# Merging the last projection with its mixer, packing the gates, and regrouping the sample value products

## The chip, the cores and the metric

One Trainium2 chip, one core, one launch of the whole program. The metric is the device time of one execution in microseconds (us), median of three runs. TensorE does the matrix products, VectorE, ScalarE and GpSimd (POOL) the element work, and SyncE starts most DMA transfers.

## The reference

One inference step of a two-layer decoder for a prompt of 256 tokens and 8 sample sequences of 4 tokens each, 288 token columns in all. Every sub-layer is `x = x + c * rmsnorm(f(rmsnorm(x)))`. Layer 0 is a half feed-forward, a mixer AB (sparse attention with a paged key/value cache, beside an RWKV-7 recurrence), and a half feed-forward; layer 1 has the mixer CD between its two feed-forwards. What the change touches, cut down:

```python
# CD mixer: retention (C) beside mLSTM (D)
z = h @ cd_w_in            # qc, kc, vc, gc, qkd, vd, ig, fg, og
qc, kc = rope(qc), rope(kc) * DK_C ** -0.5
ret_S, yc = chunked_scan(retention_chunk, ret_S, (qc, kc, vc))
qkd = silu(causal_conv(qkd)); qd, kd = split(qkd)
logi, logf = ig + b0, log_sigmoid(fg + b1)
(mC, mn, mm), hd = chunked_scan(mlstm_chunk, (mC, mn, mm), (qd, kd, vd, logi, logf))
y = concat(head_norm(yc) * silu(gc), head_norm(hd) * sigmoid(og)) @ cd_w_out
# AB mixer, sample side: p over 1024 cached and 4 new keys of each of 8 sequences
out = einsum('bqhk,bqkhd->bqhd', p, v_cached_and_new)
```

## The kernel before

Activations stand as `[128 features, 8 tiles, 288 tokens]`. A product with a weight matrix is three products of split fp32 numbers (`three_products`, lines 187 to 189): the high part of a weight by the high part of x, high by low, low by high. Weights come as "pairs" (128 x 2048 numbers, 1 MB, two output tiles of 128 features) through a ring of four slots. VectorE splits each pair (`split_pair`: a cast at line 173 and a subtraction at line 182), counted by the semaphore `pair_split`; TensorE counts the pairs it is done with in `pair_done`, and SyncE loads the next pair into a slot when that count allows.

The last projection (`cd_in_stage`) runs in one block with the stages ahead of it: eight pairs give `z` (18 tiles), then `project_values` gives the values of C and D in token-major form, each of two pairs and three token tiles (128, 128 and 32 tokens) of 24 products, and the thirteenth pair gives the eight gate rows, padded to two whole tiles of 128 features. Then the block ends with a barrier of all engines, and `cd_mix_stage` runs as a block of its own. Its order is written by hand, the same for each engine every time: gates' first steps, rotation of q and k (`rot`, line 2444 on TensorE, lines 2226 to 2228 on VectorE), the gates' scans up to `gate_arg`, the scores of C (lines 2451 and 2252 to 2254), the transposed keys (2457 and 2259), the exponents of D (2467 and 2270 to 2272, counted by `e_arg`), the retention products y (2476 to 2483), state products (`ret_states`, 2500), the convolution on VectorE (2312 and 2314), the scores of D (`query_keys`, 2509), head means (2519), and the rest of D and the head norms. `ret_values` (2279) builds the operand of `ret_states`, `ret_update` (2286) takes its result.

In mixer AB, `dsa_stage` multiplies the softmax weights of the 8 sample sequences by their value pages at line 1748: M is 32 there, and each sequence b writes its own strip of 32 rows, `32*(b % 4)`, so that two sequences' products stand side by side on TensorE. The loop goes over pairs of sequences, and small products of the recurrence stand between its parts: `decay_products` (1187 and, for the squared keys, 1190), `rate_products` (1197), `key_norms` (1205), then `value_products` (1212), which wait for `ar_done` of VectorE (lines 975 and 976). The squares at 1190 add up a square that ScalarE makes ahead of its decay sigmoids.

Of the kernel before, what the change touches and what calls it, by code (L numbers as in the profile page):

```python
# [8 lines left out]
F32 = mybir.dt.float32  # L9
I32 = mybir.dt.int32  # L10
ALU = mybir.AluOpType
# [22 lines left out]
class Chip:  # L34
# [66 lines left out]
    def sb(self, name, shape, dt=F32, ctx=None):  # L101
        return self.place(name, shape, dt, ctx)[0]

# [618 lines left out]
def project_values(c, pe, pair, tile_done):  # L722

    s = pair % RING
    hi, lo = (a[:, s:s + 2].rearrange("p s a k m -> p (s a k m)").rearrange("p (k n) -> p k n", k=KT) for a in (c.whi, c.ring_lo))
# [18 lines left out]
def ab_in_stage(c, z, vtok, idx, pre):  # L744
# [67 lines left out]
    "decay_products", "rate_products", "key_norms", "value_products", "chunk_products"))  # L812


def recurrence(c, z, ymix, idx, A, par, zlast, shared, pages):
# [3 lines left out]
    for n in ("mix_loaded", "par_loaded", "state_loaded", "shift_ready", "mixed", "lora_in", "lora_sum", "lora_out", "ld_done", "cum_done", "w_done",  # L819
# [86 lines left out]
    def rows_load(sp):  # L906

        sp.wait_ge(A["op_sum"], 8)
        sp.dma_start(pair_rows, c.ins["pair_rows"]).then_inc(S["par_loaded"], 16)
# [19 lines left out]
    def inputs(dve, ln):  # L929
# [19 lines left out]
        dve.wait_ge(S["kk_sum"], 1)  # L949
        dve.tensor_scalar(rows8, B[1][0:8, 0:NT], 1e-24, None, ALU.max).then_inc(S["kk_max"], 1)  # L950

# [4 lines left out]
        ln(last)  # L956
        dve.tensor_tensor(e3, e2, e1, ALU.subtract).then_inc(S["cum_done"], 1)
# [223 lines left out]
    def decay_products(pe):  # L1181
# [4 lines left out]
        for h in range(HP):  # L1186
            pe.matmul(free[h][:, 0:NT], wa2[0:64, h * P:h * P + P], lw[0:64, 0], start=True, stop=True).then_inc(S["lora_sum"], 1)
        pe.wait_ge(S["ld_done"], 1)
# [10 lines left out]
    def key_norms(pe):  # L1199

        pe.wait_ge(S["lora_out"], 2 * HP)
        pe.wait_ge(S["par_loaded"], 16)
# [4 lines left out]
    def value_products(pe):  # L1207

        pe.wait_ge(S["par_loaded"], 32)
# [1704 lines left out]
```

## Time and profile before

| | us |
|---|---|
| median of 3 runs (lowest, highest) | 1537.38 (1535.99, 1538.58) |
| the profiled execution | 1536.86 |
| its span in the profile | 1535.1 |
| TensorE busy | 1445.1 (94%) |
| VectorE busy | 1097.8 (72%) |
| ScalarE, POOL busy | 312.8, 332.4 |

Times of a row are counted from the span's start. "Idle before" and the engine after the arrow say how long an engine stood before that instruction and what ended it. A row of TensorE counts records: an fp32 product has two, a product of the split parts one.

### The profile page before, as it was taken

Reading aid. Unit: us, or ns where it says so; the run is one execution under the profiler, and the core shown is the slowest. Engines: PE = TensorE matmul, PEld = TensorE weight load, DVE = VectorE, ACT = ScalarE, POOL = GpSimd, SP = SyncE. Lnnn points to the kernel's source line nnn. Section 1 sums busy time; section 2 is a strip of 40 time slices with the busy share of each in tenths; the row PEclk is TensorE's granted clock in tenths of the full one; section 3 lists DMA queues with packets and bytes.
Section 4 is the critical chain, followed back from the end, with each engine's and each line's share of the span. In section 5 each row is a group of like instructions: output and inputs, shape, how many; then the busy total and the mean of one; then the engine's idle time right before and its main releaser. Section 6 shows DMA issues by size and latency. Waiting matters only on the chain. (4 is left out here: it accounts for less than half of the span.)

```text
span 1535.1 us, 28310 instructions
## 1 busy us (share of the span) xinstructions
PE 1445.1 (94%) x11482; PEld 1305.2 (85%) x11482; DVE 1097.8 (72%) x1415; ACT 312.8 (20%) x607; POOL 332.4 (22%) x282
## 2 busy tenths in 40 slices
PE   6999999997999995999999999999997896999997
PEld 6999999993343694999999999999985666999997
DVE  7977768646976726788768597767754877897764
ACT  3111101003334232222111221110201312321100
POOL 2533111001100011254321243311101002343310
PEclk9999999998998987999999999999999788999998
DMA  7442634646883103444426344354332005544152
GB/s 304 161 166 84 238 99 153 220 131 237 272 307 121 38 3 142 178 161 166 169 89 242 126 174 165 115 185 152 135 137 110 34 31 192 213 164 164 57 168 88
DMA packets 62794, 233.76 MB, mean 152 GB/s; under 512 B 9051, under 2 KB 18592, under 8 KB 45548
## 3 DMA queue, kind: packets, MB, share of 16 engines
q1 hardware_dynamic: 50426, 225.08, 41.3%
q10 hardware_dynamic: 11554, 6.37, 1.4%
q8 instruction: 69, 1.13, 0.3%
q0 software_dynamic: 720, 0.97, 0.2%
q14 instruction: 25, 0.20, 0.0%
HBM read 226.06 MB, written 6.10 MB: 151 GB/s over the span
## 5 line engine op out<-in xcount | busy, mean ns | idle before, releaser
L187 PE MATMUL psum<-x_hi_r,pair_hi 128*128 128x288 f32 x1744 | 518.5, 297 | 28.8 <-DVE ring_r L182 25.5
L189 PE MATMUL psum<-x_hi_r,ring_r 128*128 128x288 f32 x1744 | 517.6, 297 | 0.0
L188 PE MATMUL psum<-x_lo_r,pair_hi 128*128 128x288 f32 x1616 | 477.2, 295 | 0.0
L187 PEld LDWEIGHTS psum<-x_hi_r,pair_hi 128*128 128x128 f32 x1744 | 330.5, 190 | 31.4 <-DVE ring_r L182 26.4
L182 DVE TENSOR_TENSOR ring_r<-ring,pair_hi 128x2048 fp32r<-128x2048 f32 x127 | 340.2, 2678 | 4.3
L189 PEld LDWEIGHTS psum<-x_hi_r,ring_r 128*128 128x128 f32 x1744 | 329.9, 189 | 0.0
L188 PEld LDWEIGHTS psum<-x_lo_r,pair_hi 128*128 128x128 f32 x1616 | 304.9, 189 | 0.4
L187 PE MATMUL psum<-hidden_hi_r,down_hi 128*128 128x288 f32 x704 | 208.4, 296 | 0.0
L188 PE MATMUL psum<-hidden_r,down_hi 128*128 128x288 f32 x704 | 207.7, 295 | 0.0
L189 PE MATMUL psum<-hidden_hi_r,down_r 128*128 128x288 f32 x704 | 207.0, 294 | 0.0
L173 DVE CAST pair_hi<-ring 128x2048 fp32r<-128x2048 f32 x127 | 161.4, 1271 | 32.5 <-DMA ring<-in_w_gu 16.6
L652 POOL TENSOR_TENSOR hidden<-silu,up 128x288 f32 x88 | 126.7, 1439 | 122.0 <-ACT silu L578 120.2
L189 PEld LDWEIGHTS psum<-hidden_hi_r,down_r 128*128 128x128 f32 x704 | 132.6, 188 | 0.0
L188 PEld LDWEIGHTS psum<-hidden_r,down_hi 128*128 128x128 f32 x704 | 132.1, 188 | 0.0
L187 PEld LDWEIGHTS psum<-hidden_hi_r,down_hi 128*128 128x128 f32 x704 | 131.9, 187 | 0.0
L578 ACT ACTIVATE silu<-gate 128x288 f32<-128x288 f32 x88 | 39.2, 445 | 404.8 <-DVE gate L593 404.8
L182 DVE TENSOR_TENSOR down_r<-down,down_hi 128x1408 fp32r<-128x1408 f32 x64 | 117.1, 1830 | 2.2
L182 POOL TENSOR_TENSOR hidden_r<-hidden,hidden_hi_r x88 | 74.3, 844 | 204.3 <-DVE hidden_hi_r L173 204.3
L593 DVE TENSOR_TENSOR gate<-psum,rstd 128x288 f32<-128x288 f32 x88 | 40.0, 455 | 85.7 <-PE psum L189 85.3
L173 DVE CAST down_hi<-down 128x1408 fp32r<-128x1408 f32 x64 | 60.2, 941 | 49.5 <-PE psum L189 29.4
L660 POOL TENSOR_TENSOR ysq<-ysq,y 128x288 f32<-128x288 f32 x24 | 26.4, 1099 | 185.3 <-ACT y L584 185.3
L231 PE MATMUL psum<-x_hi_r,pair_hi 128*128 128x288 f32 x192 | 54.3, 303 | 11.1 <-DVE ring_r L182 11.1
(539 smaller groups left out, 1790.6 us busy)
## 6 DMA issues: line engine op xcount, KB each, us to landing
ring<-in_w_gu SPq DMA_DIRECT2D x88, 1024.0 KB, 4.9
down<-in_w_down SPq DMA_DIRECT2D x64, 704.0 KB, 4.2
ring<-in_w_ab SPq DMA_DIRECT2D x18, 1024.0 KB, 5.2
ring<-in_w_cd SPq DMA_DIRECT2D x13, 1024.0 KB, 6.1
ring<-in_cache_k SPq DMA_DIRECT2D x32, 256.0 KB, 5.3
index_keys<-in_cache_k SPq DMA_DIRECT2D x32, 256.0 KB, 4.1
index_keys<-in_cache_i ACTq DMA_DIRECT2D x64, 64.0 KB, 2.8
eight_pages_ds<-in_cache_v SPq DMA_DIRECT2D x16, 256.0 KB, 6.6
```

The costliest lines, as they stand in the source:

```text
L173: return dve.tensor_copy(hi, a)
L182: return eng.tensor_tensor(lo, a, hi.bitcast(F32), ALU.subtract)
L187: pe.matmul(out, w_hi, x_hi, start=start, stop=False)
L188: pe.matmul(out, w_hi, x_lo, start=False, stop=False)
L189: return pe.matmul(out, w_lo, x_hi, start=False, stop=stop)
L231: pe.matmul(out, c.whi[:, s, half, k], c.xhi[:, k], start=(k == 0), stop=False)
L578: act.activation(silu[:, b], gate[:, b], ACT.Silu).then_inc(silu_done, 1)
L593: dve.tensor_tensor(gate[:, b], c.banks[bank][:, 0:NT], c.rstd[:, :], ALU.mult).then_inc(gate_scaled, 1)
L652: pool.tensor_tensor(h, silu[:, b], up[:, b], ALU.mult).then_inc(c.hidden_raw, 1)
L660: pool.tensor_tensor(ysq[:, :], ysq[:, :], y2[:, n % 2], ALU.add).then_inc(ysq_added, 1)
```

## The change

Four things, all of order and placement; the arithmetic is the same.

1. `cd_in_stage` and `cd_mix_stage` become one `cd_stage` in the block of the stages ahead, with no barrier between projection and mixer. SBUF places move: `ext` (the convolution's input) goes to the end of `ymix`, `VB`, `KB`, `emj`, `hd` and `hr` go into the slots of `pair_hi` whose pair is done, and the three state loads wait for the ring slots that they use.
2. The eight gate rows come as half a pair (128 x 1024 numbers, one output tile of 24 products), right behind the eight pairs, and are taken from PSUM by 4-row products instead of as tiles of z.
3. TensorE's order: values of C tile 0, rotation, values of C tiles 1 and 2, scores of C, all values of D, then the retention products y, the gate columns, transposed keys and exponents. VectorE does the convolution ahead of `ret_values` and the exponents; POOL sets its zeros early, and those of `VB` and `KB` when their slots come free.
4. In AB the first four sequences' value products go together, four strips side by side, and the last four in pairs as before. The squared-key products (`key_squares`) stand apart from `decay_products`, ScalarE makes the decay sigmoids ahead of the square, and the small products stand at other places.

```diff
-def project_values(c, pe, pair, tile_done):
+def project_values(c, pe, pair, tile_done, tiles=(0, 1, 2)):
     pe.wait_ge(c.pair_split, pair + 2)
-    for i, (t0, n) in enumerate(TOK):
+    for i in tiles:
+        t0, n = TOK[i]
         for k in range(KT):
             cols = slice(t0, t0 + n)
-            mm = three_products(pe, c.banks[4 + i][0:n, :], c.xhi[:, k, cols], c.xlo[:, k, cols], hi[:, k], lo[:, k], k == 0, k == KT - 1)
+            s, half, k0 = (pair + k // 4) % RING, k % 4 // 2, 4 * (k % 2)
+            hi, lo = (a[:, s, half, k0:k0 + 4].rearrange("p k m -> p (k m)") for a in (c.whi, c.ring_lo))
+            mm = three_products(pe, c.banks[4 + i][0:n, :], c.xhi[:, k, cols], c.xlo[:, k, cols], hi, lo, k == 0, k == KT - 1)
...
     def lora_out(act):
-        act.wait_ge(S["kk_sq"], HP)
-        act.activation(f2[:, :, :], f1[:, :, :], ACT.Square).then_inc(S["ld_done"], 1)
...
+        act.wait_ge(S["kk_sq"], HP)
+        act.activation(f2[:, :, :], f1[:, :, :], ACT.Square).then_inc(S["ld_done"], 1)
...
+            weights_transposed(0)
+            pe.wait_ge(S["st_out"], 3)
+            pages_landed(range(4))
+            sample_values(range(4), range(4)).then_inc(S["kv_used"], 1)
+            weights_transposed(1)
+            sample_values(range(4), range(4, NPG + 1)).then_inc(S["kv_used"], 2)
+            rk.decay_products(pe)
...
+            sample_values((4, 5), range(3))
+            rk.key_squares(pe)
+            sample_values((4, 5), range(3, 6))
+            rk.rate_products(pe)
+            sample_values((4, 5), range(6, NPG + 1)).then_inc(S["kv_used"], 1)
+            pages_landed((6, 7))
+            sample_values((6, 7), range(2))
+            rk.key_norms(pe)
+            sample_values((6, 7), range(2, NPG + 1)).then_inc(S["kv_used"], 1)
             rk.value_products(pe)
...
             weights_out(0)
+            weights_out(1)
             rk.lora_inputs(act)
-            weights_out(1)
             rk.lora_out(act)
```

```diff
+        def gpsimd(pool):
+            pool.wait_ge(z_done, 1)
+            for i, pad in enumerate((negM_rows[:, :], gem_rows, kw[:, 2], vd[NS:64, 2], vd[64:P, 2])):
...
+            pool.wait_ge(c.pair_done, first + VC + 2)
+            pool.memset(VB_rows[:, :, :, :], 0.0).then_inc(S["padded"], 1)
+            pool.wait_ge(c.pair_done, first + VD + 2)
+            pool.memset(KB_rows[:, :, :, :], 0.0).then_inc(S["padded"], 1)
...
+            split_pair(c, dve, first, VD)
+            dve.wait_ge(c.pair_done, first + GATES + 1)
+            dve.tensor_tensor(gx, B[0][32:36, 0:NT], c.rstd[32:36, :], ALU.mult)
+            ln(dve.tensor_tensor(gu, B[0][0:4, 0:NT], c.rstd[0:4, :], ALU.mult))
...
-            dve.tensor_scalar(gu, z[0:4, 16], ifb[:, 0:1], None, ALU.add)
+            dve.tensor_scalar(gu, gu, ifb[:, 0:1], None, ALU.add).then_inc(gates_raw, 1)
+            split_pair(c, dve, first, VD + 1)
...
+            project_pe(c, pe, z_done, npairs, first, pre)
+            pe.wait_ge(c.pair_split, first + GATES + 1)
+            pe.wait_ge(z_done, npairs - 1)
+            for k in range(KT):
+                mm = pair_products(c, pe, B[0], first, GATES, 0, k)
+            mm.then_inc(c.pair_done, 1)
+            token_rstd_pe(c, pe, rt_sum)
+
+            values(0, (0,))
             pe.wait_ge(params.loaded, 16 * params.n)
+            pe.wait_ge(z_done, npairs)
+            pe.wait_ge(gates_raw, 1)
             for i in range(4):
                 pe.matmul(B[i][:, 0:NT], rot[:, :], z[:, i], start=True, stop=True).then_inc(S["rot_sum"], 1)
+            values(0, (1, 2))
...
-                together(nc, ab_out, ffn1, ffn2, cd_in_stage(c, z, vtok, params, pre))
-                cd_mix_stage(c, z, vtok, ymix, params)
+                together(nc, ab_out, ffn1, ffn2, cd_stage(c, z, vtok, ymix, params, pre))
```

TensorE's program in mixer AB, of before, from the new-token products that end the first pair of sequences (vtok; cmask, wmask and x_hi hold the small matrices of the recurrence's products, ring and index_keys hold value pages):

```order
L1758 MATMUL psum<-vtok,x_lo 32x512 x2
L1187 MATMUL psum<-z,cmask 128x288 x4
L1190 MATMUL psum<-shared_ds,wmask 8x288 x4
L1748 MATMUL psum<-ring,x_lo 32x512 x8
L1197 MATMUL psum<-z,cmask 128x288 x4
L1748 MATMUL psum<-ring,x_lo 32x512 x8
L1758 MATMUL psum<-vtok,x_lo 32x512 x2
L1748 MATMUL psum<-index_keys,x_lo 32x512 x8
L1205 MATMUL psum<-shared_ds,x_hi 128x288 x4
L1748 MATMUL psum<-index_keys,x_lo 32x512 x8
L1758 MATMUL psum<-vtok,x_lo 32x512 x2
```

The same place after the change, from the new-token products that end the first four sequences (the group ahead of it is eight pages for four sequences):

```order
L1752 MATMUL psum<-two_pages_ds,x_lo 32x512
L1752 MATMUL psum<-eight_pages_ds,x_lo 32x512
L1752 MATMUL psum<-ring,x_lo 32x512 x2
L1754 MATMUL psum<-vtok,x_lo 32x512 x4
L1191 MATMUL psum<-z,cmask 128x288 x4
L1752 MATMUL psum<-index_keys,x_lo 32x512 x6
L1197 MATMUL psum<-shared_ds,wmask 8x288 x4
L1752 MATMUL psum<-index_keys,x_lo 32x512 x6
L1204 MATMUL psum<-z,cmask 128x288 x4
L1752 MATMUL psum<-index_keys,x_lo 32x512 x4
L1754 MATMUL psum<-vtok,x_lo 32x512 x2
```

The decay products (z,cmask) stand behind four finished sequences instead of two; the squares (shared_ds,wmask) stand behind three pages of the next pair of sequences, and no longer right behind the decay products.

TensorE's program in the CD stage of before, behind the barrier (rot_cm is the rotation, the rows of line 2451 the scores of C, ident,z the transposed keys, ident,g_cm the gate columns, negM the exponents of D; the retention products down,vtok come next):

```order
L2444 MATMUL psum<-z_6547,rot_cm 128x288 x4
L2451 MATMUL psum<-z_6547 128x256 x2
L2451 MATMUL psum<-z_6547 128x128 x2
L2451 MATMUL psum<-z_6547 32x32 x2
L2451 MATMUL psum<-z_6547 128x256 x2
L2451 MATMUL psum<-z_6547 128x128 x2
L2451 MATMUL psum<-z_6547 32x32 x2
L2457 MATMUL psum<-ident,z_6547 128x128 x4
L2457 MATMUL psum<-ident,z_6547 32x128 x2
L2462 MATMUL psum<-ident,g_cm 128x4 x2
L2462 MATMUL psum<-ident,g_cm 32x4
L2467 MATMUL psum<-negM_cm,sel_cm 128x288 x4
```

And after the change, behind the last values of D (their third token tile):

```order
L192 MATMUL psum<-ring_r,x_hi_r 32x512
L193 MATMUL psum<-pair_hi,x_lo_r 32x512
L2499 MATMUL psum<-down,vtok_6546 128x256
L2500 MATMUL psum<-down,vtok_6546 128x128
L2499 MATMUL psum<-down,vtok_6546 128x256
L2500 MATMUL psum<-down,vtok_6546 128x128
L2502 MATMUL psum<-scs_cm,vtok_6546 128x32 x2
L2506 MATMUL psum<-qdec_cm,ring 128x4 x16
```

Here pair_hi and ring_r by x_hi_r and x_lo_r are the last values, and down,vtok and qdec,ring the retention products of the first two heads. Behind those of the other two heads stands (vtok,kw is the prompt's state product of C):

```order
L2510 MATMUL psum<-ident,g_cm 128x4 x2
L2510 MATMUL psum<-ident,g_cm 32x4
L2516 MATMUL psum<-ident,z_6545 128x128 x4
L2516 MATMUL psum<-ident,z_6545 32x128 x2
L2522 MATMUL psum<-negM_cm,sel_cm 128x288 x4
L2528 MATMUL psum<-vtok_6546,kw_cm 64x128 x8
```

Rotation and scores are gone from this place (they stand among the value products, as the diff shows for the rotation), the retention products come straight behind the values, and gate columns, transposed keys and exponents come behind them.

VectorE's program of before, from the last pair split (the thirteenth) over the two gate tiles (line 2059) and the barrier to the first rotation (tmp_cm):

```order
L173 CAST pair_hi<-ring 128x2048
L182 TENSOR_TENSOR ring_r<-ring,pair_hi 128x2048
L2059 TENSOR_TENSOR z_6547<-psum,rstd 128x288 x2
L421 UNCONDITIONAL_BRANCH
L2212 UNCONDITIONAL_BRANCH
L2218 TENSOR_SCALAR g_cm<-z_6547,ifb_cm 4x288
L2219 TENSOR_SCALAR g_cm<-g_cm 4x288
L2220 TENSOR_TENSOR g_cm<-g_cm 4x288
L2221 TENSOR_SCALAR g_cm<-g_cm 4x288
L2222 TENSOR_SCALAR g_cm<-z_6547,ifb_cm 4x288
L2226 TENSOR_TENSOR tmp_cm<-z_6547,cs_cm 128x288
L2227 TENSOR_TENSOR tmp_cm<-psum,cs_cm 128x288
```

And after the change, from the twelfth pair split:

```order
L177 CAST pair_hi<-ring 128x2048
L186 TENSOR_TENSOR ring_r<-ring,pair_hi 128x2048
L2212 TENSOR_TENSOR g_cm<-psum,rstd 4x288
L2213 TENSOR_TENSOR g_cm<-psum,rstd 4x288
L2216 TENSOR_SCALAR g_cm<-g_cm,ifb_cm 4x288
L2217 TENSOR_SCALAR g_cm<-g_cm 4x288
L2218 TENSOR_TENSOR g_cm<-g_cm 4x288
L2219 TENSOR_SCALAR g_cm<-g_cm 4x288
L2220 TENSOR_SCALAR g_cm<-g_cm,ifb_cm 4x288
L177 CAST pair_hi<-ring 128x2048
L186 TENSOR_TENSOR ring_r<-ring,pair_hi 128x2048
L2225 TENSOR_TENSOR tmp_cm<-z_6545,cs_cm 128x288
```

Before, the gate steps (g_cm) stood behind the last split and behind the barrier; now the last split stands behind them, and TensorE's rotation waits for the last of them (`gates_raw`).

## Rows read from the trace of the kernel before

**Rows 1.** The page: busy time and share of the span, by engine

```profile
PE 1445.1 (94%) x11482; PEld 1305.2 (85%) x11482; DVE 1097.8 (72%) x1415; ACT 312.8 (20%) x607; POOL 332.4 (22%) x282
```

**Rows 2.** Busy time by stretch: PE, PEld, DVE, ACT, POOL, clock, DMA, GB/s

```profile
1177.00:1200.00 23.00, 14.30 (x58) 9.82 (x59) 20.12 (x64) 7.41 (x14) 6.14 (x8) 0.63 0.35 138
```

**Rows 3.** Timeline of TensorE, 1134 to 1190: start, us, operation, [idle before]

```profile
1134.50 0.75 PE L740 MATMUL psum<-ones,rstd 1*128 1x1 f32 x6
...
1153.04 0.49 PE L187 MATMUL psum<-pair_hi,x_hi_r 128*128 128x512 f32 x1 [0.83 <-ACT vtok L2051]
...
1177.60 2.18 PE L2444 MATMUL psum<-z,rot_cm 128*128 128x288 f32 x8 [1.17 <-PEq L421]
1186.15 1.23 PE L2451 MATMUL psum<-z 64*128 64x256 f32 x4 [6.37 <-DVE z L2228]
```

**Rows 4.** Timeline of VectorE, 1141 to 1180

```profile
1141.13 2.29 DVE L182 TENSOR_TENSOR ring_r<-ring,pair_hi 128x2048 fp32r<-128x2048 f32 x1
...
1176.47 0.82 DVE L2059 TENSOR_TENSOR z<-psum,rstd 128x288 f32<-128x288 f32 x2 [15.92 <-PE psum L189]
...
1178.91 1.49 DVE L2221 TENSOR_SCALAR g_cm<-g_cm 4x288 f32<-4x288 f32 x1
```

**Rows 5.** Timeline of POOL at 1178

```profile
1178.29 1.96 POOL L2202 MEMSET VB_cm<- 128x2048 f32 x1
```

**Rows 6.** Timeline of TensorE, 1189 to 1222

```profile
1189.81 1.54 PE L2457 MATMUL psum<-ident,z 128*128 128x128 f32 x6
...
1198.88 0.74 PE L2476 MATMUL psum<-down,vtok 128*128 128x256 f32 x2
...
1203.07 1.22 PE L2476 MATMUL psum<-down,vtok 128*128 128x256 f32 x2
...
1208.38 1.15 PE L2490 MATMUL psum<-vtok,kw_cm 128*64 128x128 f32 x16
...
1214.81 1.11 PE L2509 MATMUL psum<-qk_cm 64*128 64x256 f32 x12 [1.88 <-ACT qk_cm L2418]
1215.85 3.87 PE L2519 MATMUL psum<-x_hi,ones 128*128 128x288 f32 x8
1219.64 1.94 PE L2500 MATMUL psum<-VB_cm,kw_cm 128*64 128x512 f32 x8
```

**Rows 7.** Timeline of VectorE, 1193 to 1215

```profile
1193.27 1.06 DVE L2259 TENSOR_TENSOR kw_cm<-psum,wS_cm 128x256 f32<-128x256 f32 x3
...
1199.79 0.23 DVE L2272 SCALAR_TENSOR_TENSOR Es_cm<-psum,guT_cm,lms_cm 32x32 f32<-32x32 f32 x1
...
1213.20 1.40 DVE L2286 SCALAR_TENSOR_TENSOR ring<-ring,par_cm,psum 128x512 f32<-128x512 f32 x2
```

**Rows 8.** Timeline of TensorE in mixer AB, 478 to 513

```profile
478.62 2.20 PE L1187 MATMUL psum<-z,cmask 64*128 64x288 f32 x8
...
485.29 2.20 PE L1197 MATMUL psum<-z,cmask 64*128 64x288 f32 x8
...
491.95 3.63 PE L1748 MATMUL psum<-index_keys,x_lo 128*32 128x512 f32 x16
495.51 2.20 PE L1205 MATMUL psum<-shared_ds,x_hi 8*128 8x288 f32 x8
...
510.15 2.21 PE L1212 MATMUL psum<-z,index_keys 128*128 128x288 f32 x8
```

**Rows 9.** Timeline of VectorE in mixer AB, 489 to 505

```profile
489.82 1.94 DVE L960 RECIPROCAL shared_ds<-shared_ds 8x288 f32<-8x288 f32 x1 [1.68 <-ACT shared_ds L1106]
496.30 1.91 DVE L963 TENSOR_TENSOR shared_ds<-shared_ds,psum 128x288 f32<-128x288 f32 x4 [4.54 <-PE psum L1205]
...
503.66 1.35 DVE L976 TENSOR_TENSOR ring<-z 128x1152 f32<-128x1152 f32 x1
```

**Rows 10.** The instructions of line 333: count, ns min/median/max; and one occurrence

```profile
L333 PE MATMUL psum<-ysq,ones x32: 225/238/250, 226.0 to 1523.1; 128*32 128x72 f32 x32
...
225.99 0.33 PE L333 MATMUL psum<-ysq,ones 128*32 128x72 f32 x8
```

More of the change, by code:

```diff
@@ new lines, in sample_values @@
+            def sample_values(seqs, js):
+                g = seqs[0] // 4
+                for j in js:
+                    for b in seqs:
+                        cols = slice(32 * (b % 4), 32 * (b % 4) + 32)
+                        if j < NPG:
+                            mm = pe.matmul(B[5 + g][cols, :], pts[:, g, j, cols], page_of(VALUE_SLOTS[b], j), start=(j == 0), stop=False)
+                        else:
+                            mm = pe.matmul(B[5 + g][cols, :], pts[0:NS, g, 8, cols], vtok[0:NS, 2, :], start=False, stop=True)
+                return mm
@@ new lines, in vector @@
+            split_first_pairs(c, dve, first, AHEAD + 1)
+            c.presplit = 0
+            pre.dve_rstd(dve)
+            take(0)
+            take(1)
+            split_pair(c, dve, first, 1 + AHEAD)
+            for u in range(2, npairs):
+                take(u)
+                if u + AHEAD == GATES:
+                    split_gates()
+                else:
+                    split_pair(c, dve, first, u + AHEAD)
+            split_pair(c, dve, first, VD)
+            dve.wait_ge(c.pair_done, first + GATES + 1)
@@ L2391, in _, with scalar, value_rows @@
             ln(last)
-        @block.scalar
-        def _(act):
+        def scalar(act):
+            def value_rows(w, i):
+                n = TOK[i][1]
+                if i < 2:
+                    act.wait_ge(v_sum, 2 * w + i + 1)
+                else:
+                    act.wait_ge(c.pair_done, first + (VC, VD)[w] + 2)
+                act.activation(vtok[0:n, 3 * w + i], B[4 + i][0:n, :], ACT.Copy, scale=rt[0:n, i:i + 1]).then_inc(v_done, 1)
+            pre.act_sd(act, B[6])
+            act.wait_ge(z_done, 1)
+            params.load(c, act)
+            act.wait_ge(rt_sum, 1)
+            for i, (t0, n) in enumerate(TOK):
+                act.activation(rt[0:n, i:i + 1], B[7][0:n, i:i + 1], ACT.Copy).then_inc(rt_ready, 1)
+            act.wait_ge(rt_ready, 3)
             act.wait_ge(S["gate_x"], 1)
@@ L2398, in _ @@
             act.activation(ge, ge, ACT.Ln, bias=c.ones[0:4, 0:1]).then_inc(S["gate_ln"], 1)
+            for i in range(3):
+                value_rows(0, i)
             act.wait_ge(S["gate_arg"], 1)
@@ L2453, in _ @@
                             mm.then_inc(S["s_sum"], 1)
[L2454 to L2467 removed]
+            pe.wait_ge(v_done, 3)
+            values(1, (0,))
+            values(1, (1, 2))
             pe.wait_ge(S["qdec_done"], 1)
@@ L2484, in _ @@
                 mm.then_inc(S["y_sum"], 2)
+            pe.wait_ge(S["gate_arg"], 1)
+            for i, (t0, n) in enumerate(TOK):
+                mm = pe.matmul(B[7][0:n, 4 * i:4 * i + 4], gu[:, t0:t0 + n], c.ident[0:4, 0:4], start=True, stop=True)
+            mm.then_inc(S["gut_sum"], 1)
+            pe.wait_ge(v_done, 5)
+            for i, (t0, n) in enumerate(TOK):
+                for hp in range(2):
+                    o = (i % 2) * 256 + hp * P
+                    mm = pe.transpose(B[4 + i // 2][0:n, o:o + P], K[:, hp, t0:t0 + n], c.ident[:, :])
+            mm.then_inc(S["kt_sum"], 1)
+            pe.wait_ge(v_done, 6)
+            for h in range(4):
+                if h >= 1:
+                    pe.wait_ge(S["e_arg"], max(h - 1, 1))
+                pe.matmul(B[6 + h % 2][:, 0:NT], sel[:, h], negM_rows[:, :], start=True, stop=True).then_inc(S["m_sum"], 1)
             pe.wait_ge(S["kt_out"], 1)
```

272 lines of the change are left out of this document (106 added, 166 removed).

## The prediction, on record before the changed kernel ran

> **What bounds the kernel now.** Start with the busy times: TensorE works 94% of the span, VectorE 72% [rows 1]. A change pays, then, where TensorE stands idle, where it works at the lower of its two clock levels, or where it has less work. The busy times by stretch give the place: in the 23 us behind the barrier of the CD stage TensorE is busy for 14.3 and its granted clock is 0.63 (1.2 GHz for three quarters of it), while VectorE is busy for 20.1 [rows 2]. TensorE's timeline there shows it waiting 1.17 us at the barrier and 6.37 us for the rotation [rows 3]. From the end of the values of D (1170.0, below) to the first retention products at 1198.88 [rows 6] 28.9 us pass, in which the gate pair is the only long work of TensorE; then the state product's result is taken only at 1213.20, as VectorE has the operand of `ret_states` and the convolution between [rows 7]. In mixer AB TensorE has no gap: it works through the value pages and reaches the value products of the recurrence at 510.15 [rows 8], while VectorE had waited 1.68 and 4.54 us for what stands behind those pages [rows 9].
>
> **CD stage, step by step.** Times go from the unchanged end of the eighth pair, 1134.5 [rows 3]. (a) Gates: three value tiles took (1153.04 - 0.83 - 1135.25) = 16.96 us, 5.65 each [rows 3], so the values of D ended at 1170.0 and the gate pair, 48 products, at 1176.4 [rows 4]: 6.4 us. Half of it is 3.2, so 1137.7, and 1138.4 with the row sums (0.75). the values then wait for VectorE's split of the pair before the one whose second half stands at 1141.13 [rows 4]; that split ends a microsecond or two ahead of this row, so I put a wait of 0.4 there. (b) Value tile 0 ends at 1144.5. VectorE ends the twelfth split at 1143.4 [rows 4], then come seven 4-row steps of 0.4 to 0.5 us, so `gates_raw` comes at 1146.4 and TensorE waits 1.9 us. The 1.49 us of line 2221 [rows 4] is no price for its step: a POOL memset of 1.96 us began before it and ended with it [rows 5], and after the change POOL is idle then (its zeros come behind the first pair and behind the first values, not between). With 1.49 in the sum the wait would be 3.0 us; I take 0.4 and keep 1.1 for the range.
>
> The Trainium skill ("SBUF — State Buffer", section "SBUF: two separate sides") says that VectorE in its faster modes and POOL share a port pair by an exclusive lock and one fully blocks the other. By it the new memset of `VB`, beside VectorE's gate scans, could stop one of them for up to 1.96 us. That would cost nothing here, by the slack under (d); the row's end together with the memset agrees with the page.
>
> (c) Rotation, 8 records, 2.0 of 2.18 [rows 3]: 1148.4. Value tiles 1 and 2: 1159.7. Scores, 24 records: 3.7 us at the low clock before; 12 like records took 1.11 [rows 6], so 2.2: 1161.9. Values of D, 16.96: 1178.9. (d) All that the retention products need is there: VectorE's rotation, scans and scores took from 1180.4 [rows 4] to 1193.27, 12.9 us; the operand of `ret_states`, the input copies and the convolution from 1200.0 to 1213.20, 13.2 us [rows 7]; with the last split (3.6) 29.7 us, from 1146.4 to 1176 if nothing waits, and only at 1189.5 does its next input come. So this work is hidden with some 13 us to spare; without the cover each microsecond over would count whole. The state load of C starts when the first value pair is done (1159.7), 19 us ahead of its use. (e) Retention products: the first two heads took 4.19 us, the other two 5.31, at a mixed clock [rows 6]; I take 2 x 4.2: 1187.3. Gate columns and transposed keys: 0.7 (no row shown; at most the 1.54 of the keys) and 1.5 [rows 6]: 1189.5. Weighted keys and exponents took 6.75 us, 1193.27 to 1200.02 [rows 7], with VectorE waiting for exponent products at half clock; I take 5.7: 1195.2. (f) From there TensorE's chain: `ret_states` 1.94, scores of D 1.1, means 3.87, `ret_states` 1.94 [rows 6]: 1204.0. Before, the same point was 1219.64 + 1.94 = 1221.6 [rows 6]. Nothing behind it is changed, so **CD gains 17.6 us**. Its bounds: scores 3.7 (-1.5), exponents 6.75 (-1.05), retention 9.5 (-1.1), raw gates (-1.1) give 12.9; means at the full clock (1.9 less) and keys at half their price give 20.
>
> **Mixer AB.** An fp32 product by a page has two records, and 16 records took 3.63 us [rows 8]: two strips side by side, a pair of records each 0.43. With four strips at once, eight pages of four sequences are 16 such steps, as many as two sequences took. So the first four are done when the first two were, and the decay products stand again at 478.6. Nothing before showed four value strips, but line 333 has four strips of 32 too, its records last 225 to 250 ns and eight of them 330 ns in all [rows 10]; one after another, or by twos, they would take longer. From 480.75: three pages 2.7, squares 2.1, three pages 2.7, rate products 2.15, two pages and new keys 2.9, two pages 1.7: the key norms start at 494.9, not at 495.51 [rows 8]. The other side of that step is later: from the end of the rate products (487.4) to the inverse norms (491.76) [rows 8, 9] went 4.3 us, and from the new 490.35 this gives 494.7, just in time. VectorE's chain from the first norm at 496.30 to `ar_done` at 505.0 [rows 9] is rigid and moves up by 0.6 to 504.4. TensorE has only six pages and the new keys left (6.4 us behind the norms' 2.1: 503.4), so it waits 1 us, and the value products start at 504.4, not 510.15 [rows 8]. **AB gains 5.7 us**. Bounds: 6.5 if the last norms come earlier; -1.8 if strips go by twos (below).
>
> **Sum.** 17.6 + 5.7 = 23.3. The profiled execution took 1536.86 (span 1535.1 and 1.8 around it), so 1513.6; the median is 0.5 higher, so 1514.1. I say 1514, with 1510 to 1519 as this case's own range.
>
> **Rivals.** (1) *The retention part stays at the low clock.* The clock before went up and down inside the mixer (0.74 against 1.22 us for the same two records) [rows 2, 6], and fp32 products on 64 rows and 4 columns come just behind the dense part. If all from 1178.9 to the last `ret_states` goes at the lower level: retention +2.2, keys and exponents +1.8, states and scores of D +3: +7, 1521. For it: the dips before; against it: the busy 16.96 us ahead of it. Chance 0.14. (2) *Strips go by twos.* Then the decay products come 7.6 us late (16 more steps of 0.43 and the new keys), `ar_done` at 512.0, and AB loses 1.8 instead of gaining 5.7: 1521.6. Against it are rows 10; for it, that those strips are 72 columns wide and not 512. Chance 0.10. (3) *More is won*: the clock stays up all through the mixer, means and state products at 1 us less each, D's products too: 1506. Chance 0.05. (4) *The other side: the clock falls at the wait for the raw gates.* Five value tiles (28.3 us) at half the clock cost 28.3 more, and 1514 becomes 1542; it decides as soon as 23.3 of these 28.3 are lost. For it: the clock was low behind the 1.17 and 6.37 us of idleness [rows 2, 3]; against it: the 0.83 of idleness among the same values cost nothing (the next three tiles took the same, 16.96). Chance 0.03. (5) *The merged order does not do what it says*, since a load or a slot comes so late that the values wait and the gain is gone: 0.02, as before only 0.83 us of waiting stood among them [rows 3].
>
> **Numbers.** My case 0.66, the rivals in their order 0.14, 0.10, 0.05, 0.03 and 0.02. The range 1509 to 1523 takes in (1) and (2) and leaves out (3), (4) and (5). Faster by over 0.2% (3 us, about what a measurement can tell): 0.95; within: 0.02; slower: 0.03.
>
> **What the new profile would show.** The first retention product at about 1173 of its own time (1178.9 less AB's 5.7), with no idle time before it; a wait of about 2 us ahead of the rotation, by VectorE; VectorE waiting some 13 us for the transposed keys; `ret_states` twice 18 us earlier against the eighth pair. In AB the first four sequences' records four at a time, decay products at 478.6, value products at 504.4 behind a wait of 1 us. Wrong if records of four strips lie 0.43 apart by twos, if the granted clock in the value tiles is below 1, if a wait for a load stands ahead of a value tile, or if VectorE and not TensorE ends last before the transposed keys.

## The result and the profile after

The changed kernel takes 1511.78 us (median of 4, 1509.61 to 1515.18) and the kernel before, on the same chip, 1537.37 us (1535.99 to 1538.58): ratio 0.9836, 95% interval 0.9812 to 0.986. The prediction was 1514, range 1509 to 1523. The profiled execution took 1513.73 us, its span is 1511.9.

The page's busy times, to be held against [rows 1]: TensorE is busy for 19.1 us less, and VectorE for as long as before. Only 24 records are gone, the other half of the gate pair (3.2 us); the rest is the same records in less time, as four strips run side by side in AB and more of the CD mixer runs at the full clock.

```profile
PE 1426.0 (94%) x11458; PEld 1296.0 (86%) x11458; DVE 1096.7 (73%) x1415; ACT 312.2 (21%) x607; POOL 338.9 (22%) x282
```

TensorE's timeline of the merged CD stage answers to [rows 3, 6]. The columns are start, duration, line and operation, and in brackets the idle time before:

```profile
1129.34 0.75 PE L745 MATMUL psum<-ones,rstd 1*128 1x1 f32 x6
1130.54 0.49 PE L191 MATMUL psum<-pair_hi,x_hi_r 128*128 128x512 f32 x1 [0.45 <-DVE ring_r L186]
...
1137.63 2.18 PE L2477 MATMUL psum<-z,rot_cm 128*128 128x288 f32 x8 [1.25 <-DVE g_cm L2220]
...
1150.93 2.14 PE L2484 MATMUL psum<-z 64*128 64x256 f32 x24
...
1169.88 0.59 PE L2499 MATMUL psum<-down,vtok 128*128 128x256 f32 x2
...
1177.66 0.75 PE L2510 MATMUL psum<-ident,g_cm 4*128 4x4 f32 x6
1178.34 0.88 PE L2516 MATMUL psum<-ident,z 128*128 128x128 f32 x6
1179.05 0.65 PE L2522 MATMUL psum<-negM_cm,sel_cm 128*128 128x288 f32 x2
1181.45 3.63 PE L2522 MATMUL psum<-negM_cm,sel_cm 128*128 128x288 f32 x6 [1.75 <-DVE Es_cm L2304]
1185.01 2.03 PE L2528 MATMUL psum<-vtok,kw_cm 128*64 128x128 f32 x16
...
1189.75 2.21 PE L2557 MATMUL psum<-x_hi,ones 128*128 128x288 f32 x8
```

The 6.37 us are gone that the scores waited for the rotated q and k [rows 3]: the rotation itself waits 1.25 us, the scores and the first retention product not at all. What is left in front of the states is one wait of 1.75 us in the block of exponents. The same stretches by granted clock (PEclk is the third number from the end):

```profile
1130.00:1178.00 48.00, 46.30 (x269) 33.91 (x269) 36.72 (x100) 10.69 (x20) 4.60 (x2) 1.00 0.26 93
1178.00:1187.00 9.00, 7.23 (x37) 4.85 (x38) 4.77 (x17) 8.17 (x20) 0.00 (x0) 0.62 0.00 1
1187.00:1197.00 10.00, 8.49 (x54) 4.52 (x52) 8.18 (x17) 1.92 (x5) 0.00 (x0) 1.00 0.04 15
1197.00:1228.00 31.00, 31.00 (x177) 24.11 (x177) 20.82 (x37) 4.75 (x10) 0.34 (x1) 0.67 0.10 39
```

VectorE, to be held against [rows 7]: it stands idle for 10.87 us ahead of the weighted keys, and updates the retention state at 1188.83 and 1195.00 in place of 1213.20 and 1221.63 (these times include what AB won ahead of the stage).

```profile
1179.25 1.07 DVE L2291 TENSOR_TENSOR kw_cm<-psum,wS_cm 128x256 f32<-128x256 f32 x3 [10.87 <-PE psum L2516]
...
1188.83 1.40 DVE L2309 SCALAR_TENSOR_TENSOR ring<-ring,par_cm,psum 128x512 f32<-128x512 f32 x2 [2.81 <-PE psum L2538]
...
1195.00 1.38 DVE L2309 SCALAR_TENSOR_TENSOR ring<-ring,par_cm,psum 128x512 f32<-128x512 f32 x2
```

In mixer AB, TensorE's timeline beside [rows 8]. Four strips now start within 0.01 us of each other:

```profile
466.72 1.06 PE L1752 MATMUL psum<-down,x_lo 128*32 128x512 f32 x1 [1.51 <-ACT x_lo L1844]
466.72 1.06 PE L1752 MATMUL psum<-eight_pages_ds,x_lo 128*32 128x512 f32 x1
466.73 1.07 PE L1752 MATMUL psum<-ring,x_lo 128*32 128x512 f32 x2
467.57 1.06 PE L1752 MATMUL psum<-down,x_lo 128*32 128x512 f32 x1
...
477.67 2.20 PE L1191 MATMUL psum<-z,cmask 64*128 64x288 f32 x8
...
493.81 2.20 PE L1212 MATMUL psum<-shared_ds,x_hi 8*128 8x288 f32 x8
...
503.45 3.35 PE L1219 MATMUL psum<-z,index_keys 128*128 128x288 f32 x8 [1.20 <-DVE ring L980]
```

### The profile page after: what moved, and what is told of

Its sections match the earlier page's. It is cut to its first block and busy times, and to the rows that moved or that the text cites. A ratio compares the mean times of both kernels' runs of the same rounds, so it can differ in the third digit from the quotient of the medians.

```text
span 1511.9 us, 28247 instructions
## 1 busy us (share of the span) xinstructions
PE 1426.0 (94%) x11458; PEld 1296.0 (86%) x11458; DVE 1096.7 (73%) x1415; ACT 312.2 (21%) x607; POOL 338.9 (22%) x282
## 3 DMA queue, kind: packets, MB, share of 16 engines
q10 hardware_dynamic: 11554, 6.37, 1.4%
## 5 line engine op out<-in xcount | busy, mean ns | idle before, releaser
L191 PE MATMUL psum<-x_hi_r,pair_hi 128*128 128x288 f32 x1736 | 516.0, 297 | 28.8 <-DVE ring_r L186 25.6
L186 DVE TENSOR_TENSOR ring_r<-ring,pair_hi 128x2048 fp32r<-128x2048 f32 (+1 forms) x127 | 337.5, 2658 | 4.3
L177 DVE CAST pair_hi<-ring 128x2048 fp32r<-128x2048 f32 (+1 forms) x127 | 160.7, 1265 | 19.1 <-DMA ring<-in_w_gu 16.6
L177 DVE CAST down_hi<-down 128x1408 fp32r<-128x1408 f32 x64 | 62.1, 970 | 49.2 <-PE psum L193 30.5
L664 POOL TENSOR_TENSOR ysq<-ysq,y 128x288 f32<-128x288 f32 x24 | 31.9, 1330 | 179.7 <-ACT y L588 179.7
```

Of the source, the lines that this page charges most:

```text
L177: return dve.tensor_copy(hi, a)
L186: return eng.tensor_tensor(lo, a, hi.bitcast(F32), ALU.subtract)
L191: pe.matmul(out, w_hi, x_hi, start=start, stop=False)
L664: pool.tensor_tensor(ysq[:, :], ysq[:, :], y2[:, n % 2], ALU.add).then_inc(ysq_added, 1)
```

## The experiments

Medians in us; "before" is the kernel before, measured beside the others on the same chip. The table has three groups by their "before", each from another chip, and the kernel before alone differs by 4.6 us between them; across groups the ratios are the fairer comparison. A ratio and its interval come from the record and are not the quotient of the two medians; the two differ by up to 0.0013 (2 us). An interval is 3 to 4 us to each side, that of AB alone 2.

| kernel | median (range, runs) | before | ratio, 95% |
|---|---|---|---|
| AB change alone | 1530.81 (1527.04 to 1534.13, 10) | 1536.33 | 0.9963, 0.995 to 0.9977 |
| CD change alone | 1517.91 (1512.4 to 1523.3, 5) | 1536.33 | 0.987, 0.9851 to 0.9889 |
| strips by twos | 1519.5 (1517.88 to 1525.27, 6) | 1536.33 | 0.9903, 0.9884 to 0.9922 |
| rotation, scores behind all values | 1527.16 (1522.17 to 1535.1, 7) | 1536.33 | 0.9937, 0.9914 to 0.9961 |
| rotation one tile later | 1511.59 (1508.92 to 1513.39, 5) | 1534.32 | 0.9846, 0.9826 to 0.9865 |
| convolution twice | 1509.29 (1508.41 to 1514.39, 5) | 1534.32 | 0.984, 0.9819 to 0.9861 |
| retention products among exponents | 1509.95 (1506.14 to 1512.35, 5) | 1534.32 | 0.9841, 0.9823 to 0.986 |
| gate columns first | 1512.12 (1505.12 to 1517.93, 6) | 1534.32 | 0.9855, 0.983 to 0.988 |
| the changed kernel again | 1510.61 (1509.84 to 1517.71, 5) | 1538.9 | 0.9828, 0.9801 to 0.9854 |
| three edits together | 1507.83 (1506.75 to 1510.96, 5) | 1538.9 | 0.9797, 0.978 to 0.9815 |
| gates twice | 1513.0 (1511.42 to 1514.84, 5) | 1538.9 | 0.9838, 0.9819 to 0.9856 |
| retention products early | 1517.26 (1512.55 to 1518.79, 5) | 1538.9 | 0.9854, 0.9831 to 0.9877 |

**AB change alone, CD change alone.** The first kernel has the change's edits to `recurrence` and the AB mixer only, the second all others only.

> The kernel before with the change in the AB stage alone (four sequences' strips at once, the key norms' squares behind the sigmoids, its loads' own counter). My theory: the two stages' gains add up and have nothing to do with each other. In the profile of the changed kernel the work up to the end of AB's layer has been brought forward by 8.33 us, of which I put 5.7 down to the strips and the waits and the rest to stretches at half clock that the recurrence's chunk part didn't fall into this time. If that is right: 5.7 to 8.3 us under before, ratio 0.9946 to 0.9963, with the clock in the chunk part deciding where. The rival (part of the gain up to CD comes by way of the CD change, for example through where tensors lie) would leave less than 4 us here.

> The kernel before with the change in the CD stage alone. From the profile of the changed kernel: retention states 18.3 us earlier, of which 3.4 are given back in D's part at half clock, so 14.9 us net in that execution. If the give-back belongs to the change, 1522.4 us (ratio 0.990); if it is the chance of that one execution, 17.6 us as in my sum, 1519.8 us (0.9886).

AB alone gains 5.5 us and CD alone 18.4, together 23.9, where both edits together gained 25.6: they add up within the intervals, and the rival that AB's gain hangs on CD's is out. AB's 8.3 us in the profile of the changed kernel were in part a draw: the point that it was read at (the row sums behind the gates) stood at 1129.34 there, and in the profiles of eight later kernels with the same code up to there between 1127.36 and 1133.11. The four of them that ran on one chip lie within 0.8 us, three on another within 3.5, so some of this spread may belong to the chips. The profile of AB alone even shows the point 10.35 us earlier than before (1124.15), for 5.5 in the medians.

**Strips by twos.**

```diff
-            sample_values(range(4), range(4)).then_inc(S["kv_used"], 1)
+            sample_values((0, 1), range(4)).then_inc(S["kv_used"], 1)
             weights_transposed(1)
-            sample_values(range(4), range(4, NPG + 1)).then_inc(S["kv_used"], 2)
+            sample_values((0, 1), range(4, NPG + 1)).then_inc(S["kv_used"], 1)
+            sample_values((2, 3), range(NPG + 1)).then_inc(S["kv_used"], 1)
```

> The changed kernel with the value products of the first four sequences by twos again, everything else of the change left in. By my sum four strips at once take the step time of two, so that the second pair's 17 steps of 0.427 us cost 7.3 us: 7.3 us slower than the changed kernel. The rival of the prediction (strips by fours are no faster than by twos) would make it even with the changed kernel. Where the transposed weights' copies were late, part of the 7.3 could be hidden, down to 5.

7.7 us over the changed kernel's first median, 10 by the two ratios. Its timeline of TensorE has the two strips of a step, the decay products and the value products:

```profile
467.10 1.06 PE L1752 MATMUL psum<-down,x_lo 128*32 128x512 f32 x1 [1.51 <-ACT x_lo L1845]
467.11 1.06 PE L1752 MATMUL psum<-eight_pages_ds,x_lo 128*32 128x512 f32 x1
467.95 1.06 PE L1752 MATMUL psum<-down,x_lo 128*32 128x512 f32 x1
...
485.97 2.20 PE L1191 MATMUL psum<-z,cmask 64*128 64x288 f32 x8
...
511.75 2.18 PE L1219 MATMUL psum<-z,index_keys 128*128 128x288 f32 x8 [1.19 <-DVE ring L980]
```

A step lasts as long with two strips as with four (0.85 at the lower clock level in both). From the first strip to the decay products it is 18.87 us, in the changed kernel 10.95: 7.92 more, all of it still there at the value products. The fours are worth more than AB's whole change. How much the rest of it costs (norms and squares in new places) the medians can't tell, but the profiles can: from the second group of transposed weights (472.95 before, 472.33 here) to the value products it is 37.2 us before and 39.4 here, 2.2 us lost, where the bound of rival 2 had 1.8.

**Rotation and scores behind all value products.**

```diff
             values(0, (0,))
-            ... rotation ...
             values(0, (1, 2))
-            ... scores ...
             pe.wait_ge(v_done, 3)
             values(1, (0,))
             values(1, (1, 2))
+            ... rotation, scores ...
```

> The changed kernel with the rotation and the scores behind all value products, in place of among them. My sum says that the waits of the rotation (VectorE's rope, some 9 us from rotation to last key) and of the scores' masks (3 us) are what the value products cover, so 8 to 14 us slower than the changed kernel. The rival is that VectorE's own chain (it idles for 10.87 us ahead of the weighted keys in the changed kernel) is the spare that takes it up: then VectorE's work moves but TensorE only waits for rope, and the loss is 4 to 6 us.

15.4 us slower than the changed kernel by the medians, beyond both expectations; its seven executions lie 10 to 23 us over that kernel's median. The profiled one is the slowest of them, 1535.10 us. TensorE's timeline there:

```profile
1168.96 2.10 PE L2483 MATMUL psum<-z,rot_cm 128*128 128x288 f32 x8
1175.08 3.73 PE L2489 MATMUL psum<-z 64*128 64x256 f32 x24 [4.02 <-DVE z L2227]
1182.96 1.19 PE L2500 MATMUL psum<-down,vtok 128*128 128x256 f32 x2 [4.15 <-DVE scs_cm L2264]
...
1197.64 1.20 PE L2511 MATMUL psum<-ident,g_cm 4*128 4x4 f32 x6
```

Two waits, of 8.2 us together, stand there as expected. The rest of this execution's loss is the clock: it fell to 1.2 GHz in the first wait (0.60 in 1174 to 1176) and stayed there to 1208, so that scores took 3.73 for 2.14 and the retention products 14.7 for 7.8 us. From the row sums to the first state product it is 17.3 us more than in the changed kernel, of which some 10 are the clock. In the other executions it must be less, as the fastest is only 10.4 us over the changed kernel's median; none of them has a profile. In the median the waits cost about twice their length, and the clock's share of that is argued from the one profile.

This kernel also bounds what the rest of the CD change is worth, without the cover. It is 3.7 us under AB alone, measured beside it: no barrier, half a gate pair and the convolution's new place together. Neither the barrier nor the convolution's place was tried alone.

**Rotation one tile later.** `values(0, (1,))` ahead of the rotation, `values(0, (2,))` behind it.

> The changed kernel with the rotation behind value tile 1 in place of behind value tile 0. In the changed kernel TensorE waits 1.25 us there for VectorE's raw gates. My theory: the tile covers it, and the rope (VectorE, some 9 us) still ends before the last value tile and the scores' turn comes or shortly after, so 1.2 us faster than the changed kernel. The rival: with one tile (8 us) in place of two between rotation and scores, the scores wait for the last rope and VectorE's later work moves by 8 us, for which it has 10.87 us to spare; then 0 to 2 us slower. Both are near what the runs can tell apart; the profile's waits ahead of rotation and scores decide.

Even with the changed kernel (ratio 0.9846, against 0.9836 and 0.9828 of the changed kernel's two measurements). The wait of 1.25 us is gone and the first retention product comes 37.8 us behind the first value product in place of 39.3: 1.5 gained, as the theory had it. But in this execution the retention products took 10.07 us, as the clock fell in them, and nothing of the gain was left at the states. The rival's late scores didn't come.

**Convolution twice.**

```diff
-            for i in range(4):
+            for again in range(2):
+              if again:
+                  ln(last)
+              for i in range(4):
```

> The changed kernel with the convolution computed twice over (9.2 us more on VectorE, the same output). VectorE idles for 10.87 us behind it in the changed kernel, so my theory expects the time of the changed kernel within the measurement, with the idle time ahead of the weighted keys down to 1.7 us. The rival (the convolution's end also sets the SiLU table load on ScalarE, and with it the exponentials and the scores' weights) expects 2 to 4 us more.

Not measurably slower (0.984). VectorE's row ahead of the weighted keys takes up all of the 9.3 us, and rotation to first state product lasts 47.4 us in both kernels:

```profile
1177.56 1.07 DVE L2294 TENSOR_TENSOR kw_cm<-psum,wS_cm 128x256 f32<-128x256 f32 x3 [1.55 <-PE psum L2519]
```

**Retention products among the exponents; gate columns first.** The first kernel issues the products of heads 0 and 1 behind the first exponent product and those of heads 2 and 3 behind the third, with ScalarE's copies of them behind its exponentials. The second:

```diff
 # VectorE
+            dve.wait_ge(S["gut_sum"], 1)
+            ... the two copies to guT, then_inc(S["guT_out"], 1) ...
             dve.wait_ge(S["kt_sum"], 1)
             ... weighted keys ...
 # TensorE
-                if h >= 1:
-                    pe.wait_ge(S["e_arg"], max(h - 1, 1))
+                if h == 1:
+                    pe.wait_ge(S["guT_out"], 1)
+                if h >= 2:
+                    pe.wait_ge(S["e_arg"], h - 1)
```

> The changed kernel with the retention products (7.8 us) moved from ahead of the exponents to among them: the first two heads' behind the first exponent product, the others' behind the third. TensorE waits for VectorE there (1.75 us in the changed kernel) and the last 6 us go at half clock. If the wait is what costs, 1.75 to 3 us faster than the changed kernel. If the retention products' small operations are themselves what the clock falls behind, the block costs more at half clock than the wait saves, and the result is even or up to 2 us slower. ScalarE's copies of the retention output then come behind its exponentials.

> The changed kernel with the copies of the transposed gate columns ahead of the weighted keys on VectorE, and with the second exponent product waiting for these copies in place of the first head's finished exponents. The wait of 1.75 us in front of that product, which covers weighted keys, copies and three additions on VectorE, should go. Clock theory: without the pause TensorE's clock holds through the block, and its 5.9 us of exponent and state products at half clock shrink too, 3 to 4 us faster in all. Slot theory: the next wait, for the second head's exponents, is VectorE's own chain, which doesn't get shorter; then 0 to 1 us faster.

By the medians both are even with the changed kernel. In the profiles both shorten the way from rotation to first state product (47.38 us) as the wait theory said: to 45.27 and 45.06. Of the second, TensorE's timeline and the clock of the block:

```profile
1175.79 0.75 PE L2511 MATMUL psum<-ident,g_cm 4*128 4x4 f32 x6
1176.48 0.87 PE L2517 MATMUL psum<-ident,z 128*128 128x128 f32 x6
1177.19 1.14 PE L2525 MATMUL psum<-negM_cm,sel_cm 128*128 128x288 f32 x4
1179.33 1.56 PE L2525 MATMUL psum<-negM_cm,sel_cm 128*128 128x288 f32 x4 [1.00 <-DVE Es_cm L2305]
1180.82 1.15 PE L2531 MATMUL psum<-vtok,kw_cm 128*64 128x128 f32 x16
```

```profile
1175.80:1180.80 5.00, 3.94 (x22) 2.50 (x20) 3.60 (x14) 4.85 (x12) 0.00 (x0) 1.00 0.01 2
```

The wait of 1.75 became one of 1.00 for the next head, 0.75 won (slot theory), and the clock stayed at 1.00, so that the exponent products took 2.6 us in place of 4.2. That is what the clock theory says, but 2.3 us in all is short of its 3 to 4. The profile is of the fastest of six executions, which lie 12.8 us apart; whether the clock holds because of the edit is not shown, and the medians can't show 2.3. The profile of the other kernel is of its fastest execution too.

**The changed kernel again, and three edits together.** The second joins the later rotation, the gate columns first with exponents 0 and 1 back to back, and the retention products around exponents 2 and 3.

> The changed kernel itself, once more, beside the three others. 1508 to 1515 us as before. In the profiled executions so far the same code between the rotation and the first state product took 47.4 us three times and 51.6 us once, where TensorE's clock had fallen at the start of the retention products; I expect that the place at which the clock falls, and with it up to 4 us, differs between executions of one kernel.

> Rotation behind value tile 1, gate columns copied first, exponents 0 and 1 back to back and the retention products around exponents 2 and 3, all in one kernel. By the profiles of the three alone: 1.5 us ahead of the scores, 2.1 to 2.3 us in the block of exponents (the two that touch it don't add up, since both remove the same wait), so 3.6 us under the changed kernel measured beside it. If the clock falls earlier for the shorter waits' sake or by chance, it gives 2 to 4 of them back, and the result is even with the changed kernel.

The changed kernel took 49.0 us this time from rotation to first state product, 47.4 in the first profile and 51.6 with the CD change alone, with the same instructions. Most of that is where in the retention products the clock fell. These are the same 90 or so products in three kernels (of the changed one, then CD alone, then the changed one again):

```profile
1169.90:1177.70 7.80, 7.80 (x90) 7.23 (x88) 0.00 (x0) 1.39 (x3) 1.80 (x1) 1.00 0.74 278
```

```profile
1177.80:1188.80 11.00, 11.00 (x90) 10.06 (x89) 0.00 (x0) 1.39 (x3) 1.80 (x1) 0.69 0.54 197
```

```profile
1173.50:1182.90 9.40, 9.40 (x89) 8.48 (x88) 0.00 (x0) 1.39 (x3) 1.80 (x1) 0.82 0.60 231
```

The three edits together are the fastest kernel measured: 2.8 us under the changed one beside it, four of its five runs below all five of the other's, though the two intervals overlap (0.978 to 0.9815 and 0.9801 to 0.9854). TensorE's timeline has no idle time from the gate columns to the first state product:

```profile
1171.40 0.75 PE L2496 MATMUL psum<-ident,g_cm 4*128 4x4 f32 x6
...
1173.77 0.59 PE L2510 MATMUL psum<-down,vtok 128*128 128x256 f32 x2
...
1182.04 0.75 PE L2525 MATMUL psum<-negM_cm,sel_cm 128*128 128x288 f32 x2
1182.72 1.31 PE L2540 MATMUL psum<-vtok,kw_cm 128*64 128x128 f32 x16
```

From the first value product (1133.48) to the first state product it is 49.2 us, in the changed kernel 54.5. Of these 5.2, 2.8 reach the median. Some of it is given back right behind: the clock falls at 1183.6, and the next state products (line 2550) take 3.5 us, where those of the changed kernel took 2.0.

**Gates twice.** The 24 products of the gate columns are issued once more, into a bank that nobody reads.

> The changed kernel with the gate columns' 24 products issued twice, the first time into a bank that nobody reads. This is the time on TensorE that packing the gates into half a pair saves: 24 products of 0.133 us, 3.2 us slower than the changed kernel by my sum. The rival: VectorE's split of the half pair and its raw gate steps are what the stage waits for there (a wait of 0.45 us behind the gates, 1.25 us ahead of the rotation), then 24 products more cost 1.5 to 2.8 us.

2.4 us slower than the changed kernel beside it by the medians, 1.5 by the ratios, which is less than the intervals. The profile speaks for the rival: the waits of 0.45 and 1.25 us that VectorE causes are gone, so 3.2 - 1.7 = 1.5 is what TensorE has to pay there. Packing the gates is worth about 2 by this, not the 3.2 that its products took.

**Retention products early.** They stand between tile 0 and tiles 1 and 2 of D's values.

> The changed kernel with the retention products ahead of the last two value tiles in place of behind all of them. They wait there for the scores' masks on VectorE (about 3 us) behind the value tile that stays ahead, and behind the last tile the transposes then wait for ScalarE's scaled copies (0.7 us each), which the retention products cover in the changed kernel: 1 to 2 us slower. Against it: the small retention products then stand between two stretches of wide ones, and if TensorE's clock falls behind a run of small products, it holds here; then up to 3 us faster.

6.7 us slower than the changed kernel beside it by the medians and 4 by the ratios, though the two intervals overlap: neither end of what was expected. No wait stands ahead of these products, and the clock fell all the same, 5 us into them, right behind the first run of 32 records of 4 columns. It stayed down in the first 4 us of the wide value products behind (0.63 us a record in place of 0.40). TensorE's timeline:

```profile
1160.79 1.95 PE L2503 MATMUL psum<-qdec_cm,ring 64*128 64x4 f32 x32
...
1163.47 1.06 PE L2496 MATMUL psum<-down,vtok 128*128 128x256 f32 x2
...
1165.88 3.58 PE L2503 MATMUL psum<-qdec_cm,ring 64*128 64x4 f32 x32
1169.38 0.79 PE L191 MATMUL psum<-pair_hi,x_hi_r 128*128 128x512 f32 x1
1169.98 0.63 PE L192 MATMUL psum<-ring_r,x_hi_r 128*128 128x512 f32 x1
```

The products took 10.6 us for 7.8 and the two tiles 13.3 for 11.3: 4.8 us lost here, of which 1.1 came back at the exponents. From the row sums to the first state product this profile is 3.7 us longer than the changed kernel's first and 2.1 longer than its second, less than the 6.7 of the medians; the difference stays open. So in this execution wide products around the small ones didn't hold the clock; they paid for its fall.

## Why the prediction was right, step by step

It was right in its mechanism and in its sum: 23.3 us forecast, 25.6 measured, and 5.5 and 18.4 for the stages alone, where 5.7 and 17.6 were forecast. The sum is nearer than its terms: in the CD stage some were too low by 1.8 us together, (e) and what stands right behind it, and others too high by 3.0, so that part of the closeness is luck. Times of the new profile are brought to those of the prediction below by adding 8.33, what the work ahead had gained there.

- **(a) Gates.** Half a pair took 3.17 us as forecast: the row sums behind it stand 5.16 us earlier than in [rows 3], so the end of the eighth pair came 5.16 + 3.17 = 8.33 earlier. The wait behind them is 0.45 (forecast 0.4). The other half, now gone, is worth about 2 on the path, since waits for VectorE would fill part of its room; the sum had these waits as terms of its own.
- **(b) Raw gates.** 1.25 us of wait, forecast 1.9. The step with 1.49 us in [rows 4] (line 2221 there, 2219 in the changed kernel) took 0.29 with no memset beside it.
- **(c) Values, rotation, scores.** The scores took 2.14 (forecast 2.2), the first retention product stands at 1169.88, with the 8.33 at 1178.2 (forecast 1178.9), and no load, slot or state was waited for: rival 5 is out.
- **(d) Slack.** 13 us forecast, 10.87 in the row, and 9.3 us of it were filled without loss.
- **(e) Retention and exponents.** 7.8 us for 8.4, but 6.75 for the block that was put at 5.7: it is bound by the wait for the first head and by the lower clock, as before. In the one profile with the gate columns first the way from rotation to states is 2.3 us shorter. The term was undersized by 1.05, and the sum had no place for the state products of line 2528: 0.8 us of them, at half clock, stand behind the last exponents.
- **(f) States, scores of D, means.** They came at full clock (1.00 in 1187 to 1197), the means at 2.21 for 3.87, which the sum had kept at its old price; a wait of 0.58 for VectorE ahead of the second state product wasn't in it. 18.3 us gained at the second retention update, 17.6 forecast.
- **Behind it** the prediction said that nothing changes. In the profiled execution 3.4 us were given back in D's part, where the clock was 0.67; CD alone gained 18.4 in the medians and its interval ends at 0.9889, short of the 0.990 that a give-back of 3.4 would mean, so it was that execution's draw.
- **AB.** The four strips go in the time of two: rival 2 is out, at 7.9 us. Norms at 493.81 (494.9), value products at 503.45 (504.4) behind a wait of 1.20 (1). That is 6.7 us earlier than before; 0.95 of them are the first eight steps, more of which ran at the lower clock before, and 5.7 are left, as forecast. These products then took 3.35 us in place of 2.21, at half clock.
- **The memset of `VB`.** The prediction had it beside the gates' scans; it came beside the input copies (last section). It cost nothing by the slack, as the prediction had it.
- **Rivals 1, 3 and 4.** The lower clock did come into the retention products, over part of them and not all, by 0 to 3.2 us in the profiles (6.9 with the rotation behind the values): a partial rival 1. Rival 3 didn't come, as the clock fell in the exponents and in D's part. Rival 4 never happened at the wait for the raw gates (clock 1.00 from 1120 to 1162 in all profiles with the changed CD stage), but its mechanism is real: in the profile of the kernel with the rotation behind the values the clock fell in a wait of 4.0 us, and some 10 us were lost by it.

What stays open is what decides the moment at which the clock falls within the retention products. It fell 4 to 5 us behind their start in five of the profiles, each time shortly behind the first run of 32 records of 4 columns, and about 10 us behind it in five others, when most kernels are in the block of exponents. One of these five is the kernel of the three edits together, with no idle time ahead. With the gate columns first it fell only in D's part.

## What to carry to other kernels

Put the operations whose result passes through another engine (rotation, rope, scores, masks) among long products that need nothing, and price a wait at its length plus what a fallen clock does to the stretch behind it: here 8 us of waits became 15 in the median and over 20 in the slowest execution. Read where a profile's gain comes from against several executions before it is booked, since the same code shifted by up to 5.8 us between them and between chips, and look which of the executions the profile is of; only the medians of each half of a change told its worth (5.5 where one profile said 8.3 and another 10.4). When slots of a fixed count run side by side in TensorE's rows or columns, fill all of them: four strips of 32 took the time of two.

## What the hardware showed

- Four column strips of 32 with 512 columns each run side by side. A step, one record of each strip, takes 0.43 us at the full clock with two strips and with four (two in 470.95 to 471.38, four in 471.01 to 471.44 of the two profiles).
- VectorE's copies beside a POOL memset. Two timelines of the changed kernel, VectorE's and POOL's: a copy of 128x24 takes 0.16 us, the one beside the memset 1.88, and the memset 2.79 in place of the 1.80 of an equal one with VectorE idle.

```profile
1150.90 0.67 DVE L2251 COPY ymix<-z 128x1024 f32<-128x1024 f32 x1
...
1151.92 0.17 DVE L2254 COPY ymix<-z 128x32 f32<-128x32 f32 x1
1152.01 1.88 DVE L2253 COPY ymix<-convT_cm 128x24 f32<-128x24 f32 x1
```

```profile
1151.06 2.79 POOL L2177 MEMSET VB_cm<- 128x2048 f32 x1 [53.64 <-PE psum L193]
1170.10 1.80 POOL L2179 MEMSET KB_cm<- 128x2048 f32 x1 [16.25 <-PE psum L193]
```

  The slack of 10.87 us hid both. The Trainium skill ("SBUF — State Buffer", section "SBUF: two separate sides") has one of the two engines stop the other while it holds their shared ports. The rows agree with it: the memset began while the copy of 128x1024 ran and took 0.99 us more than the equal one, as if it had stood still to 1152.05; the copy that began at 1152.01 ended at 1153.89, 0.04 us behind the memset. Why the small copies between them went ahead of the memset isn't shown.
- TensorE's clock can fall while TensorE is busy without a pause. In the profiles of the retention products early, of CD alone, of the changed kernel again and of the later rotation it went from 1.00 to 0.50 within 1.3 us behind the first run of 32 small fp32 records (4 columns each), at 1163.4, 1182.0, 1177.5 and 1171.4, while products of 128 and 256 columns ran. In other profiles the same run passed at 1.00, so the run alone doesn't decide it.
